# Fourteen row slots in the expert phase, and other turns for the background rows beside the two group phases

## The reference

```python
def first_block(x, mem, ...):
    ...                     # convolution, differential attention, cross attention
    hf = rmsnorm(x, norm_ffn_g[l])
    x = x + peer_ffn(hf, w_pq[l], sub_keys[l], peer_u[l], peer_v[l])
    return rmsnorm(x, final_g)

def peer_ffn(h, w_pq, sub_keys, peer_u, peer_v):
    ...                     # for each token and each of 8 heads: the 16 best of 128 x 128 experts, and gates g
    ue = peer_u[experts]
    ve = peer_v[experts]
    act = gelu(einsum('td,thkd->thk', hc, ue))
    return einsum('thk,thkd->td', g * act, ve)

def hybrid_layer(x, w_in, w_out, ln_g, ln_b, rel_bias, topk):
    proj = einsum('bsd,dn->bsn', x, w_in)
    qA, kA, vA, gA, qB, kB, vB, gB, qI, kI, wI = split(proj)
    oA = stick_breaking_attention(qA, kA, vA)          # 8 heads
    oB = dsa_sparse_attention(qB, kB, vB, qI, kI, wI, rel_bias, topk)   # 8 heads, top 128 keys by index scores
    mix = concatenate([oA * silu(gA), oB * silu(gB)])
    return layer_norm(ALPHA * x + mix @ w_out, ln_g, ln_b)
```

## Time and profile before

| | |
|---|---|
| time, median of 3 runs (lowest, highest) | 3143.04 us (3140.9, 3146.79) |
| the profiled execution: time, span | 3149.22 us, 3147.4 us |
| mean granted TensorE clock | 0.875 |
| busy: PE, DVE, ACT, POOL | 2449.2, 1758.7, 892.3, 972.7 us |
| expert phase, rows from the first gather to the last add | 907 to 1692 us |
| group phase of tiles 0 and 1, with the rows of tile 2 | 1692 to 2290 us |
| group phase of tile 2, with the rows of tile 3 | 2290 to 2817 us |
| group phase of tile 3 | 2817 to 3147 us |
| moved by DMA | 803.85 MB, mean 255 GB/s |

### The profile page before, as it was taken

One profiled execution on the slowest core, in us unless ns is written; L12 is line 12 of the kernel. 1 busy time (PEld: TensorE's weight loads), 2 busy tenths in 40 slices (PEclk: granted clock), 3 DMA queues, 4 the chain that ended last, 5 costly groups with the idle time before them and its releaser, 6 DMA issues. The chain is left out here.

```text
span 3147.4 us, 30198 instructions
## 1 busy us (share of the span) xinstructions
PE 2449.2 (78%) x9721; PEld 1632.5 (52%) x9721; DVE 1758.7 (56%) x3652; ACT 892.3 (28%) x1720; POOL 972.7 (31%) x691
## 2 busy tenths in 40 slices
PE   6997999869767887878775896787657466559897
PEld 4776878757633333333332564465436334337574
DVE  3434310142158777787763498477659857874242
ACT  3443222133212121221211343143224313223232
POOL 2323554433212333333342244133313523420101
PEclk9998999979988998989898997888778678769899
DMA  4222333321148989988998699799879999975543
GB/s 161 80 63 67 93 107 93 107 81 54 60 179 335 361 344 369 364 338 347 365 391 350 241 403 380 270 350 361 339 281 388 407 365 354 377 280 190 210 171 141
DMA packets 255850, 803.85 MB, mean 255 GB/s; under 512 B 18302, under 2 KB 138518, under 8 KB 190183
## 3 DMA queue, kind: packets, MB, share of 16 engines
q0 software_dynamic: 73728, 536.90, 42.9%
q1 hardware_dynamic: 181991, 265.35, 24.2%
HBM read 793.36 MB, written 14.07 MB: 257 GB/s over the span
## 5 line engine op out<-in xcount | busy, mean ns | idle before, releaser
L1308 POOL DMA_INDIRECT gathered<-in_peer_rows,experts x512 | 600.3, 1172 | 1286.3 <-DVE x_res L2420 673.7
L1424 PE MATMUL peer_banks<-gathered,peer_diags 128*128 128x512 f32 x1024 | 508.8, 655 | 171.7 <-ACT peer_diags L1484 171.7
L1424 PEld LDWEIGHTS peer_banks<-gathered,peer_diags 128*128 128x128 f32 x1024 | 210.8, 211 | 459.4 <-issue 459.2
L1587 DVE CUSTOM_DVE_ANT_0 peer_product<-gathered,early_nat 128x1024 f32<-128x1024 f32 x256 | 307.3, 1224 | 142.2 <-DMA gathered<-in_peer_rows,experts 141.2
L78 PE MATMUL group_banks<-group_x_t,group_ring 128*128 128x128 f32 (+1 forms) x2016 | 347.5, 337 | 18.8 <-ACT group_mix_t L2333 12.8
L78 PEld LDWEIGHTS group_banks<-group_x_t,group_ring 128*128 128x128 f32 x2016 | 314.4, 213 | 50.3 <-ACT group_mix_t L2333 13.2
L2406 DVE CUSTOM_DVE_ANT_0 gathered<-gathered,late_nat 128x1024 f32<-128x1024 f32 x256 | 322.8, 1264 | 27.0 <-DMA gathered<-in_peer_rows,experts 24.1
L2420 DVE SCALAR_TENSOR_TENSOR x_res<-gathered,group_weights,x_res 128x1024 f32<-128x1024 f32 x256 | 334.4, 1306 | 2.7 <-DVE group_weights L2412 0.3
L2057 PE MATMUL group_banks<-group_ring,group_x_t 128*128 128x512 f32 x512 | 228.7, 601 | 8.5 <-DMA group_ring<-in_weights 8.5
L1477 ACT ACTIVATE peer_acts<-peer_dots 128x2 f32<-128x2 f32 x128 | 26.0, 203 | 605.0 <-DVE peer_dots L1587 604.8
L2057 PEld LDWEIGHTS group_banks<-group_ring,group_x_t 128*128 128x128 f32 x512 | 96.9, 193 | 127.0 <-issue 115.4
(11 more groups left out here) (320 smaller groups left out, 4021.0 us busy)
## 6 DMA issues: line engine op xcount, KB each, us to landing
group_ring<-in_weights SPq DMA_DIRECT2D x270, 512.0 KB, 5.7
mixer_wq<-in_w_in SPq DMA_DIRECT2D x24, 512.0 KB, 4.1
mixer_wk<-in_w_in SPq DMA_DIRECT2D x24, 512.0 KB, 5.5
peer_w<-in_w_pq SPq DMA_DIRECT2D x8, 1024.0 KB
gathered<-in_peer_rows,experts POOLq DMA_INDIRECT x512
diff_wv<-in_w_in SPq DMA_DIRECT2D x8, 512.0 KB, 4.0
conv_wb<-in_w_in SPq DMA_DIRECT2D x8, 512.0 KB, 4.0
merge_w<-in_w_conv_out SPq DMA_DIRECT2D x8, 512.0 KB, 3.5
```

The lines of the kernel that those rows point to most:

```text
L1308: nc.gpsimd.indirect_dma_start(m.gathered[:, slot, :], None, A["peer_rows"], bass.IndirectOffsetOnAxis(ap=at, axis=0))\
L1424: last = nc.tensor.matmul(ps[:, ACC[unit % 2] + half, :], diags[:, r % DIAGS, :], rows[:, r % SLOTS, D + half * BANK:D + (half + 1) * BANK ...
L1587: nc.vector.tensor_tensor_reduce(out=product[:, r % 2, :], in0=rows[:, r % SLOTS, 0:D], in1=nat[t // 2][:, t % 2, :], scale=1.0, scalar=0. ...
```

## The change

It has three parts. The expert phase gets fourteen slots: the ten of `gathered`, which live through the group phases, and four in a buffer `early_gathered` of its own. Rows below 256 take the fourteen in turn, counted so that row 255 has slot 13; later rows take the ten in turn, from slot 0. How often a slot has been used before is now counted from a list. Second, `layer_points` gets more and smaller places: `values` becomes `kI`, `qI` 0 and 1, and `v0` for each tile; `gate0` becomes `soft0` and `g0` for each tile; `v1` for each tile is new and stands in the last stick-breaking pair; `keep` loses weight, and `gate1` is preceded by `g1` for each tile. ScalarE's `gelus` and VectorE's `rows` are called at each. Third, a place `first` opens each layer: in layer 0 before the input scaling, with weight 40, in layer 1 with 8.

```diff
-    LOT, SLOTS = 2, 10
+    LOT, SLOTS, EARLY_SLOTS = 2, 10, 14
...
+EARLY_ROWS = FIRST_ROW[GROUPS[1]]
+SLOT_OF = [(r - EARLY_ROWS) % Rows.EARLY_SLOTS if r < EARLY_ROWS else (r - EARLY_ROWS) % Rows.SLOTS for r in range(ROWS_IN_ALL)]
+def users_before(r):
+    return [n for n in range(r) if SLOT_OF[n] == SLOT_OF[r]]
+USERS_BEFORE = [users_before(r) for r in range(ROWS_IN_ALL)]
+def row_buffer(m, r):
+    slot = SLOT_OF[r]
+    return m.gathered[:, slot, :] if slot < Rows.SLOTS else m.early_gathered[:, slot - Rows.SLOTS, :]
+def row_landed(r):
+    return 16 * (len(USERS_BEFORE[r]) + 1)
+def row_freed(r):
+    return USERS_BEFORE[r][-1] + 1
...
+        m.early_gathered = sb("early_gathered", [P, Rows.EARLY_SLOTS - SLOTS, 2 * D])
...
-                    if r >= SLOTS and r % LOT == 0:
-                        pool.wait_ge(m.row_added, r + LOT - SLOTS)
+                    if r >= Rows.EARLY_SLOTS and r % LOT == 0:
+                        pool.wait_ge(m.row_added, row_freed(r + LOT - 1))
                     gather(nc, A, m, r)
...
-    points = [(("start",), 6), (("values",), 34 * NT)]
+    points = [(("first",), 8), (("start",), 6), (("kI",), 4 * NT), (("qI", 0), 7 * NT), (("qI", 1), 7 * NT)]
+    points += [(("v0", t), 14) for t in tiles]
     points += [(("scores", t, h), 3) for t in tiles for h in range(1, HEADS, 2) if t >= 1]
-    points += [(("pair0",), 7 * NT), (("gate0",), 6 + 14 * NT)]
+    points += [(("pair0",), 7 * NT), (("soft0",), 4)] + [(("g0", t), 14) for t in tiles]
     for p in range(PAIRS):
         points += [(("stick", p, n), 4 + 2 * NT) for n in range(4)]
-    points += [(("keep",), 14 * NT), (("gate1",), 10 + 21 * NT)]
+        if p + 1 == PAIRS:
+            points[-2:-2] = [(("v1", t), 14) for t in tiles]
+    points += [(("keep",), 4)] + [(("g1", t), 14) for t in tiles] + [(("gate1",), 10 + 7 * NT)]
...
-        points = [((l,) + p, w) for l in range(LAYERS) for p, w in layer_points(beside)]
+        points = [((l,) + p, 40 if p == ("first",) and l == 0 else w) for l in range(LAYERS) for p, w in layer_points(beside)]
...
+                done = gelus((0, "first"), done)
                 inverse_roots(0)
                 for l in range(LAYERS):
+                    done = gelus((l, "first"), done)
...
                     copy_index_keys(l)
-                    copy_index_queries(l, 0)
-                    copy_index_queries(l, 1)
-                    copy_values(l, STICK)
-                    done = gelus((l, "values"), done)
+                    done = gelus((l, "kI"), done)
+                    for n in range(2):
+                        copy_index_queries(l, n)
+                        done = gelus((l, "qI", n), done)
+                    done = copy_values(l, STICK, done)
...
+                done = rows((0, "first"), done)
                 scale_input()
                 each = DSA_TOPK // 8 // PAIRS
                 for l in range(LAYERS):
+                    done = rows((l, "first"), done)
                     done = rows((l, "start"), done)
-                    done = rows((l, "values"), done)
+                    done = rows((l, "kI"), done)
+                    for n in range(2):
+                        done = rows((l, "qI", n), done)
+                    for t in tiles:
+                        done = rows((l, "v0", t), done)
```

More of the change, by code:

```diff
@@ L1306, in gather @@
     at = m.experts[:, t, h * TOPK + k:h * TOPK + k + 1]
[L1307 to L1314, removed]
+    nc.gpsimd.indirect_dma_start(row_buffer(m, r), None, A["peer_rows"], bass.IndirectOffsetOnAxis(ap=at, axis=0))\
+        .then_inc(m.row_loaded[SLOT_OF[r]], 16)
 def peer_stage(nc, A, m, h_t, nat):
@@ L1424, in add_row @@
                         last = nc.tensor.matmul(ps[:, ACC[unit % 2] + half, :], diags[:, r % DIAGS, :],
-                                                rows[:, r % SLOTS, D + half * BANK:D + (half + 1) * BANK], start=k == 0, stop=k == TOPK - 1)
+                                                row_buffer(m, r)[:, D + half * BANK:D + (half + 1) * BANK], start=k == 0, stop=k == TOPK - 1)
                     last.then_inc(m.row_added, 1)
@@ L2263, in copy_values @@
                         nc.scalar.activation(values[half][:, t, :], bank, ACT.Copy).then_inc(proj_copied, 1)
+                        done = gelus((l, f"v{half}", t), done)
+                    return done
                 def rectify(l, n):
@@ L2296, in stick_weights, with gates @@
                     nc.scalar.activation(work[:, 1, :, :], ps[:, pair_banks(u):pair_banks(u) + 2, 0:SC], ACT.Exp).then_inc(weighted, 1)
-                def gates(l, half):
+                def gates(l, half, done):
                     if half == STICK and searched:
@@ L2312, in gates @@
                         nc.scalar.activation(share[:, n, :], share[:, n, :], ACT.Exp, scale=-1.0).then_inc(gate_step, 1)
+                        done = gelus((l, f"g{half}", t), done)
+                    return done
                 def sparse_weights(l, u):
@@ L2401, in dot @@
                     t = row_source(r)[0]
-                    row = m.gathered[:, r % Rows.SLOTS, 0:D]
-                    dve.wait_ge(m.row_loaded[r % Rows.SLOTS], row_landed(r))
+                    row = row_buffer(m, r)[:, 0:D]
+                    dve.wait_ge(m.row_loaded[SLOT_OF[r]], row_landed(r))
                     if lot >= bg.RING and n % bg.LOT == 0:
@@ L2587, in _ @@
                     soft(l, 0)
-                    done = rows((l, "gate0"), done)
+                    done = rows((l, "soft0"), done)
+                    for t in tiles:
+                        done = rows((l, "g0", t), done)
                     for u in range(PAIRS):
@@ L2596, in _ @@
                             soft(l, u + 1)
+                        else:
+                            for t in tiles:
+                                done = rows((l, "v1", t), done)
                         done = rows((l, "stick", u, 2), done)
@@ L2602, in _ @@
                     gated_stick(l)
+                    for t in tiles:
+                        done = rows((l, "g1", t), done)
                     done = rows((l, "gate1"), done)
@@ L2646, in persistent @@
     m.value_store = nc.dram_tensor("value_store", [LAYERS, 2, T, P, D // 2], F32, kind="Internal").ap()
-    m.row_loaded = [nc.alloc_semaphore(f"row_loaded{k}") for k in range(Rows.SLOTS)]
+    m.row_loaded = [nc.alloc_semaphore(f"row_loaded{k}") for k in range(Rows.EARLY_SLOTS)]
     m.row_added = nc.alloc_semaphore("row_added")
```

19 lines of the change are left out of this document (9 added, 10 removed).

## The result

The changed kernel takes **3016.01 us** (median of 4 runs, 3011.91 to 3018.5) where the kernel before takes 3144.91 (4 runs, 3140.9 to 3151.87): the ratio is 0.9586, with a 95% interval of 0.9568 to 0.9604. That is 129 us less; forecast were 100 less, 3043 us, and the measured time lies in the range, 1 us inside the edge of the 3015 to 3070 that got the chance of 0.62. Its profiled execution has a span of 3012.9 us at a mean granted clock of 0.888.

The account below looks back on a forecast made before the run. No single engine was taken as always busy: a too shallow row buffer bound the expert phase, Gelu and score waits the group openings. Terms -54 - 33 - 19 + 4 + 1 + 1 = -100 us gave 3043 us, range 2995 to 3112.

Parts of the forecast that it names:

- Rival 1: Expert phase: slots buy nothing, since memory already gives its limit or TensorE lags; 3097 us, chance 0.12.
- Rival 2: Group phases: gains given back as early rows compete with the weight ring for DMA; 3079 us, chance 0.15.
- fourteen slots: Expert phase: a deeper row buffer keeps the DMA busy, -54 us, bounds -67 and -15.
- finer turns in the openings: Group-phase openings: earlier Gelus and rows cut TensorE's waits at score products, -33 us, between -10 and -44.
- finer turns elsewhere: Value and gate tiles: same work spread finer, 0; more Gelu bursts on ScalarE, +1 us.
- rows first, with fewer dense steps: Group phases: fewer VectorE steps behind the openings, -19 us, against later input scaling, +4 and +1.
- the scaling that comes later: Group starts: steps queued on VectorE ahead of input scaling, +1 us in the first group, +4 in the second.
- the ceiling: Expert phase: most the slots could save, 670 us going from DMA share 0.89 to 0.99, 67 us.
- Together 11 to 12: Expert phase: slots needed, counting 5 rows stored, 4 under work and 2 to 3 in flight.
- Gelu bursts: Group phases: bursts grow from 58 to 63, +14 us of ScalarE, mostly covered, taken as +1 us.
- Rival 3: Group phases: slower, ScalarE's Gelus wait for rows and hold up projection copies TensorE needs; 3182 us, chance 0.06.
- Rival 4: Whole kernel: no change, Rival 1 and Rival 2 together, openings' saving spent on rows that come first; chance 0.05.

Follow-up runs that it names:

- e1: Changed kernel with fourteen slots but the turn places and weights of the kernel before, no rows first: 3068.62 us.
- e11: Fourteen slots with finer turns only in the openings of the group phases, all else as in the kernel before, no rows first: 3039.19 us.
- e3: Changed kernel without rows first (weight 0 at the place `first` in both layers), fourteen slots and finer turns kept: 3038.60 us.
- e2: Changed kernel with ten slots instead of fourteen, finer turns and rows first kept: 3102.76 us.
- e4: Kernel before (ten slots, old turns) with only the place `first` added, weights 40 and 8: 3122.54 us.
- e5: Control: changed kernel's code, slot numbering and buffers, but ten slots and the old turns: 1.0004 of the kernel before.
- e7: e5 with sixteen diagonals instead of eight: 1.0005 of the kernel before.
- e6: Changed kernel with twelve slots instead of fourteen: 3040.77 us.
- e10: Fourteen slots, old turns, VectorE's expert searches for heads 1 to 7 left out: 3043.78 us.
- e9: Ten slots, old turns, VectorE's expert searches for heads 1 to 7 left out: 3056.99 us.
- e8: Changed kernel with a weight ring of eight blocks instead of six in group phases of one tile: 3018.21 us.
- e12: Changed kernel with first-group weights raised, 60 instead of 40 at `first` and 76 instead of 56 at `out`: 3007.35 us.

## Why the prediction came out as it did

**The shape was right.** The range of 2995 to 3112 also held the times of rivals 1 and 2 (3097 and 3079), so that the time lies in it says little; the parts say more. By medians the change comes apart like this, put in one after the other (e1 from before; e11 from e1; e3 from e11; after from e3):

```
term                               predicted    measured
fourteen slots                        -54         -73.7
finer turns in the openings           -33         -29.4
finer turns elsewhere (bursts: +1)     +1          -0.6
rows first, with fewer dense steps    -14         -22.6
sum                                  -100        -126.3
```

That the measured parts add up to 126.3, near the 128.9 of the result, is no check: each step starts where the last one ended, and the difference is that of the kernel before on two chips. Each part is uncertain by 8 to 13 us, and in another order the parts would have other sizes (e2, e4). The forecast's -14 is -19 for the fewer steps and +5 for the scaling that comes later.

**The slots, the term that was mis-sized.** The step that was off is the ceiling: "670 us at 0.89, if they went to 0.99, would save 670 x 0.10 = 67 us", and the four fifths taken of it. The phase went past the ceiling, from some 776 us (the ten-slot profiles, e5) to 696, because share and bytes don't rise together; of the time's gain, 63 to 79 us, that can't be said. In the earlier trace rows the share rises by 11% from the heavy part to the tail and the rate by 16%. By bytes the 670 us at 352 GB/s become 670 x 352 / 403 = 585, 85 us less, and the profiled phases differ by 80 to 87. The rate of the tail, 408, was in the forecast's own rows and would have given 670 x (1 - 352 / 408) = 92 as the ceiling. The reduction to four fifths stood on TensorE's bursts and its 8 diagonals; e7 shows that with ten slots the diagonals limit nothing.

**How many slots.** "Together 11 to 12" is too low: e6 shows that twelve are not enough. "Fourteen are enough, by this count" is not shown either way. e10 shows that the searches still cost 18 us with fourteen; whether more slots would win them back was not run. The cause that the forecast named, VectorE's searches as the stretch in which no row is used, is shown by e9: take them out and ten slots do as well as fourteen. What the count left out was not measured singly; it took a mean head, and in the changed kernel, of the sixteen stretches of 5 us between 930 and 1605 us that lie under 0.97, eight fall within the 75 us from 955:

```profile
965.00:970.00 5.00, 5.00 (x10) 2.15 (x9) 4.85 (x20) 1.57 (x6) 0.76 (x1) 0.77 0.64 270
...
1020.00:1025.00 5.00, 5.00 (x11) 2.06 (x10) 5.00 (x11) 1.61 (x6) 1.88 (x2) 0.81 0.73 262
```

**The openings** came out within 4 us by the medians, with some 12 us of noise on the difference. The score waits fell by 37.2 us (44.1 to 6.9, forecast 33), since three waits of at most 2.8 us are left, not 2.8 in each of four openings. In e11 29 us of it show as time, with score waits of 11.5.

**Rows first** gave 22.6 us where 14 were forecast, a difference at the edge of the noise (11 us), and two of its costs were left out. The one that was priced came out: TensorE stands 35.95 us before the second group's first turn, against 33.07 in e3, +2.9 where +4 was forecast, and 26.76 against 26.57 in the first, +0.2 for +1:

```profile
1632.34 3.77 PE L2043 MATMUL group_banks<-ident,x_res 128*128 128x128 f32 x16 [26.76 <-DVE x_res L2476]
1910.10 1.97 PE L2043 MATMUL group_banks<-ident,x_res 128*128 128x128 f32 x8 [7.35 <-ACT group_x_t L2264]
2196.12 1.97 PE L2043 MATMUL group_banks<-ident,x_res 128*128 128x128 f32 x8 [35.95 <-DVE x_res L2476]
```

These rows are the changed kernel's. In e3 the second group's first turn reads:

```profile
2205.92 1.97 PE L2043 MATMUL group_banks<-ident,x_res 128*128 128x128 f32 x8 [33.07 <-DVE x_res L2476]
```

The first cost left out is the row at 1910.10, in layer 1 of the first group. There "first" puts a Gelu on ScalarE ahead of the copies of the turned input: ScalarE loads the table at 1898.43, waits 8.22 us for VectorE's dots, and TensorE, whose two banks are full, waits 7.35 us. The five other runs with "first" in this layer (e2, e4, e6, e8, e12) have this wait too, of 5.0 to 7.4 us; the kernel before and e3 have 0.36 us there. The second is the DMA: the second group's waits for weight blocks are 17.6 us longer than in e3.

On the other side stands what VectorE has less to do behind the openings. By the sum of the weights e3 has 8 and 75 steps done when the values are copied in the first group's two layers, the change 13 and 77, and in the second group 7 and 73 against 14 and 77. That makes 13 steps fewer in the dense rest than in e3, some 30 us at 2.34 (the forecast's 11 and 26 us are counted from the old turns). How much of them shows as time, which the forecast put at three quarters, can't be read from a difference of 22.6 us with 11 us of noise and these costs in it.

**Gelu bursts:** 63, as counted. Their number shows no cost: e11, with 61, is not faster than e3, with 63. Where one stands can cost, as above. The groups of instructions of the changed kernel on ScalarE (busy us, mean ns, idle before) have:

```profile
L2252 ACT ACT_TABLE_LOAD x63 | 80.8, 1283 | 1.1
```

**The rivals.** Rival 1, slots buy nothing, falls to e1. The changed kernel holds 403 GB/s for 698 us and e10 418 for 570 us; the Trainium skill, "DMA: Bandwidth & Descriptors", "Where 436 GB/s comes from", has some 358 GB/s as the memory side's bound for a core, and these runs do not agree. Rival 2, the ring, is there in part: TensorE's waits for weight blocks rose from 8.5 us to 28.2 in both groups together. The longest:

```profile
2226.86 7.08 PE L2082 MATMUL group_banks<-group_ring,group_x_t 128*128 128x512 f32 x12 [13.41 <-DMA group_ring<-in_weights]
```

It didn't take the gain, and e8 shows that the wait can't be bought off with two more blocks. By e3, 17.6 of the second group's 28.0 us come with rows first. Rival 3, ScalarE's bursts before the copies: its mechanism is there once, in the 7.35 us above, at a copy that it didn't name. At those it named there is little: no wait of TensorE for a value or gate copy is among the twelve largest groups of its waits for ScalarE and VectorE in the two groups; the smallest of those is 2.7 us. Rival 4 needed 1 and 2. What the forecast said the profile would show is there, and of the signs of being wrong the ring waits of rival 2. The slots' part is stronger than said: a phase of 696 us instead of 730, and a share of 0.99 instead of 0.97.

## What to carry to other kernels

Take the ceiling of a transfer-bound phase from bytes and GB/s, not from the DMA share, and let a stretch of the same trace at its full rate give the rate. A buffer whose producer and consumer both wait in turn may be too shallow, as this one was; a count of its depth from the mean came out too low here, so try two sizes, because the step from ten to twelve slots was worth 61 us and the next one 19. Work put ahead of a phase's first dependency gained 22.6 us here for 3 us at that dependency, but look at what each engine's queue then holds up: one Gelu ahead of the copies cost TensorE 7 us.

## What the hardware showed that was not expected

- DMA share and rate don't go together: 354 GB/s at 0.89 (398 per unit of share), 403 at 0.99 (407), 418 at 1.01 (414). Why a share of 1 then stands for more bytes was not tested.
- From 1085 to 1145 us the changed kernel's one core moved 422 GB/s on average (twelve stretches of 5 us, 416 to 428), above the 408 of the tail in the earlier trace rows.
- The ten-slot kernels' expert phases spread over 11 us (772.4 to 783.1), those of the fourteen-slot ones with searches over 3.5 (694.2 to 697.7). Without the 783.1 of the kernel before it is 4.4, so that the deeper buffer makes the phase steadier is not shown.
